# Even mixer of a two-block network: the gates' reciprocals in four pieces, the projection tiles in quarters over the recurrence's steps, and the logarithms of the attention's norm moved ahead

## The chip, the cores and the metric

The kernel runs on one core of a Trainium2 chip. The metric is the device time of one execution in microseconds (us), lower is better. TensorE (PE) has two levels of clock, 2.4 and 1.2 GHz; the profile gives the level granted in a stretch as a share, 1.00 or 0.50. DVE is VectorE, ACT is ScalarE, POOL is GpSimd.

## The reference, cut to what matters

The whole network is two blocks; the change lies in the even mixer of the second (512 tokens, width 1024, everything float32). Cut to what matters here:

```
def even_mixer(x, w_in, w_out, ...):
    h = x @ w_in
    qa, ka, va, hq, hf, hi, hg = jnp.split(h, cuts, axis=-1)
    o_a = diff_attention(qa, ka, va, ...)      # ends in an rms_norm * (1 - 0.2)
    o_b = hgrn2(hq, hf, hi, hg, lb, hg_g)
    return jnp.concatenate([o_a, o_b], axis=-1) @ w_out

def hgrn2(hq, hf, hi, hg, lb, out_g):          # 4 heads, chunks of 64 tokens
    ...
    a = einsum('nbhtk,nbhsk->nbhts', qc * exp(b - b_mid), kc * exp(b_mid - b))
    a = where(tril, a, 0)
    o_intra = einsum('nbhts,nbhsv->nbhtv', a, vc)
    def step(state, xs):                       # 8 chunks, one after the other
        o_inter = einsum('bhtk,bhkv->bhtv', qo, state)
        state = dc[..., None] * state + einsum('bhsk,bhsv->bhkv', ks, vv)
    ...
    o = rms_norm(o, out_g) * silu(hg)
```

`silu(hg)` is hg / (1 + exp(-hg)); this is "the gate" below.

## The kernel before

Each engine has a program of its own (`even_pe`, `even_act`, `even_dve`, `even_pool`), written out by hand; an engine works strictly in the order of its program, and semaphores (`wait_ge`, `then_inc`) join them. No scheduler moves anything.

**Projection.** `x @ w_in` is done in 28 tiles t = 0 to 27 (128 output columns x 512 tokens), each of 24 matmuls: 8 parts k of the inner dimension times three products (high and low halves of weights and input). Before a tile's matmuls ACT makes the high half of its weights (`act_hi`, L242) and DVE the low half (`dve_lo`, L249). `ev_tile` does a tile in one go, `ev_half(t, h)` does one half of it (12 matmuls, L3214 to L3216). Tiles 20, 21, 24, 25 are the values `hi` of heads 0 to 3, tiles 22, 23, 26, 27 the gates `hg`. A tile lands in a PSUM bank (`ev_bank`: B[6], or B[7]), and the next tile of that bank waits until it has been read. Values go to SBUF by ACT (`values`), are turned by PE (`ev_vtr`) and copied by DVE (`turn`).

**Gates.** `gates(t)`: ACT computes exp(-g) from PSUM into the buffer `vt` (L3499). DVE adds one (L3691), takes the reciprocal of the whole 128x512 tile (L3693) and multiplies by the tile in PSUM into `hg` (L3695), which frees the bank.

**The attention's norm.** PE has summed the squares of the four attention heads into banks B[0] to B[3]. ACT takes the logarithm (L3533) and then exp(-0.5 ...) (L3538); DVE scales the heads with it (L3765, L3768). The banks B[0] to B[5] are also those of the recurrence, so PE waits for the fourth logarithm (`da_ac.at("ln", 3)`) before the recurrence.

**Recurrence.** `hgrn` runs two heads side by side, first heads 0 and 1 (steps s = 1 to 9), then heads 2 and 3 (s = 1 to 11; steps 10 and 11 of heads 0 and 1, their norms, come right behind step 1 of the second pair). `head(h, 0)` prepares a head: two subtractions on DVE (L3718, L3720), five exponentials on ACT, four products on DVE (L3723 to L3727), three memsets. Step 1: PE turns the keys (L3379), ACT copies them (`kst`, L3470), PE forms the first two score blocks (L3366, L3367), DVE copies their lower triangles (`intra`, L3711, L3713). Step s = 2 to 9 is chunk c = s - 2: PE multiplies keys and values (L3390), score block and values (L3395) and the state and queries (L3397); DVE updates the state `sh` (L3743); ACT copies the output (L3475). At s = 3, 5 and 7 (odd steps below) PE also forms the next two score blocks, and DVE copies their triangles (four copies a head); the second of these blocks waits for the bank which the state update of the same step frees:

```
            elif 2 <= s < 10:
                ...
                if c % 2 and c < 7:
                    intra(c + 1)
                    intra(c + 2)
```

After the heads' parts of each step every engine calls its `between(s)` (first pair) or the second function (second pair), where other work is put. Before the change PE does half a tile at each of s = 2 to 9, tiles 24 to 27. ACT and DVE prepare heads 2 and 3 at s = 3 and s = 5. The gates 26 and 27 are whole on DVE at s = 8 and 9. The second pair has nothing beside it on PE and DVE; ACT copies parts of the result into `xh` (L3562), and POOL makes `xl` of six of them (L3792). Then come norms (L3408), the last products (L3750, L3753), and the output projection `pj_evo` (L257 to L259).

## Time and profile before

| what | value |
|---|---|
| median of 3 runs | 3791.18 us (3788.5 to 3801.71) |
| the profiled execution's own time | 3791.59 us |
| its span | 3789.8 us |
| granted TensorE clock, mean over the span | 0.952 |
| PE busy / weight loads busy | 3436.3 us (91%) / 2733.8 us (72%) |
| DVE / ACT / POOL busy | 2059.0 (54%) / 1491.5 (39%) / 224.9 us (6%) |

The stretch that the change touches is about 119 us long: it runs from the end of tile 23 at 2408.2 us to the first matmul of the output projection at 2526.97 us. The rows further down are read like this: a row of a timeline gives start, duration, engine, line, operation, output <- inputs, and in brackets how long the engine stood idle before it and whose end it waited for.

### The profile page before, as it was taken

Reading aid. Unit: us, or ns where it says so; the run is one execution under the profiler, and the core shown is the slowest. Engines: PE = TensorE matmul, PEld = TensorE weight load, DVE = VectorE, ACT = ScalarE, POOL = GpSimd, SP = SyncE. Lnnn points to the kernel's source line nnn. Section 1 sums busy time; section 2 is a strip of 40 time slices with the busy share of each in tenths; the row PEclk is TensorE's granted clock in tenths of the full one; section 3 lists DMA queues with packets and bytes.
Section 4 is the critical chain, followed back from the end, with each engine's and each line's share of the span. In section 5 each row is a group of like instructions: output and inputs, shape, how many; then the busy total and the mean of one; then the engine's idle time right before and its main releaser. Section 6 shows DMA issues by size and latency. Waiting matters only on the chain.

```text
span 3789.8 us, 59831 instructions
## 1 busy us (share of the span) xinstructions
PE 3436.3 (91%) x24660; PEld 2733.8 (72%) x24660; DVE 2059.0 (54%) x3388; ACT 1491.5 (39%) x2714; POOL 224.9 (6%) x455
## 2 busy tenths in 40 slices
PE   6888899999989958778899999789999989799999
PEld 4755788888866647676688887566888666568886
DVE  4377443334476747774544456655445655454446
ACT  5478342222246533334433334424333534343334
POOL 0011000000000014333100000000000000000000
PEclk8999999999999968999999999879999999899999
DMA  4122123321134677764222221111222211112221
GB/s 191 45 79 90 57 111 141 137 100 67 56 112 144 173 192 173 170 165 148 78 90 99 100 100 67 37 62 67 100 100 89 77 66 45 50 67 91 98 100 56
DMA packets 294414, 378.22 MB, mean 100 GB/s; under 512 B 240449, under 2 KB 243393, under 8 KB 259585
## 3 DMA queue, kind: packets, MB, share of 16 engines
q1 hardware_dynamic: 280912, 328.78, 27.0%
q10 hardware_dynamic: 13232, 45.61, 3.6%
q8 instruction: 198, 3.24, 0.4%
q14 instruction: 72, 0.58, 0.0%
HBM read 330.30 MB, written 44.06 MB: 99 GB/s over the span
## 4 chain that ended last, share of the span: by engine, by line
PE 79%; DVE 9%; ACT 6%; issue 3%; DMA 2%; POOL 0%; SPq 0%; ACTq 0%; DVEq 0%; POOLq 0%
PE ps L257 19%; PE ps L258 18%; PE ps L259 18%; PE ps L1368 1%; PE ps L1370 1%; PE ps L1369 1%; PE ps L339 1%; DVE wlo L249 1%; PE ps L803 1%; PE ps L789 1%; PE ps L2889 1%; PE ps L2213 1%; PE ps L2195 1%; PE ps L2223 1%; PE ps L3877 1%
## 5 line engine op out<-in xcount | busy, mean ns | idle before, releaser
L242 ACT ACTIVATE whi<-panel 128x512 fp32r<-128x512 f32 (+1 forms) x517 | 435.2, 842 | 585.7 <-PE ps L259 574.0
L249 DVE TENSOR_TENSOR wlo<-panel,whi 128x512 fp32r<-128x512 f32 (+1 forms) x517 | 495.8, 960 | 235.5 <-ACT whi L242 226.2
L257 PE MATMUL ps<-dh,whi 128*128 128x512 f32 (+1 forms) x1280 | 474.6, 371 | 0.0
L258 PE MATMUL ps<-dh,wlo 128*128 128x512 f32 (+1 forms) x1280 | 471.7, 369 | 0.0
L259 PE MATMUL ps<-dl,whi 128*128 128x512 f32 (+1 forms) x1280 | 471.4, 368 | 0.0
L257 PE MATMUL ps<-xh,whi 128*128 128x512 f32 x1088 | 443.2, 407 | 25.1 <-DVE xl L2930 19.2
L258 PE MATMUL ps<-xh,wlo 128*128 128x512 f32 x1088 | 429.2, 395 | 0.0
L259 PE MATMUL ps<-xl,whi 128*128 128x512 f32 x1088 | 428.8, 394 | 0.0
L257 PE MATMUL ps<-hh,whi 128*128 128x512 f32 (+1 forms) x960 | 352.8, 367 | 26.0 <-DVE hl L460 25.9
L258 PE MATMUL ps<-hh,wlo 128*128 128x512 f32 (+1 forms) x960 | 340.3, 354 | 0.0
L259 PE MATMUL ps<-hl,whi 128*128 128x512 f32 (+1 forms) x960 | 339.8, 354 | 0.0
L1161 DVE TENSOR_TENSOR relu<-relu 128x512 f32<-128x512 f32 (+1 forms) x160 | 102.2, 639 | 367.4 <-ACT relu L1136 367.4
L257 PEld LDWEIGHTS ps<-dh,whi 128*128 128x128 f32 x1280 | 241.4, 189 | 46.6 <-issue 3.3
L257 PEld LDWEIGHTS ps<-xh,whi 128*128 128x128 f32 x1088 | 207.6, 191 | 88.1 <-issue 23.0
L259 PEld LDWEIGHTS ps<-dl,whi 128*128 128x128 f32 x1280 | 241.3, 189 | 40.6
L258 PEld LDWEIGHTS ps<-dh,wlo 128*128 128x128 f32 x1280 | 241.5, 189 | 40.2
L1136 ACT ACTIVATE relu<-ps 128x512 f32<-128x512 f32 (+1 forms) x160 | 88.7, 554 | 427.6 <-PE ps L259 427.6
L258 PEld LDWEIGHTS ps<-xh,wlo 128*128 128x128 f32 x1088 | 208.3, 191 | 45.8 <-issue 5.1
L259 PEld LDWEIGHTS ps<-xl,whi 128*128 128x128 f32 x1088 | 207.6, 191 | 44.2
L257 PEld LDWEIGHTS ps<-hh,whi 128*128 128x128 f32 x960 | 183.4, 191 | 67.1 <-issue 27.7
L258 PEld LDWEIGHTS ps<-hh,wlo 128*128 128x128 f32 x960 | 184.3, 192 | 27.6 <-issue 4.6
L259 PEld LDWEIGHTS ps<-hl,whi 128*128 128x128 f32 x960 | 183.9, 192 | 25.1
(537 smaller groups left out, 5763.7 us busy)
## 6 DMA issues: line engine op xcount, KB each, us to landing
panel<-in_w SPq DMA_DIRECT2D x246, 1024.0 KB, 4.8
late<-s_fe ACTq DMA_DIRECT2D x16, 1024.0 KB, 5.7
late<-s_fe ACTq DMA_DIRECT2D x48, 256.0 KB, 3.9
s_fe<-x SPq DMA_DIRECT2D x24, 256.0 KB, 3.3
late<-s_fe ACTq DMA_DIRECT2D x8, 768.0 KB, 6.2
s_fe<-xx SPq DMA_DIRECT2D x16, 256.0 KB, 2.7
s_fe<-ctx SPq DMA_DIRECT2D x24, 128.0 KB, 2.9
s_ia<-panel SPq DMA_DIRECT2D x24, 128.0 KB, 4.0
```

The lines of the kernel that those rows point to most:

```text
L242: e.activation(unit(u)[0][:, 0:kc, :], w, ACT.Copy).then_inc(*w_hi.up(u))
L249: e.tensor_tensor(lo[:, 0:kc, :], w, hi[:, 0:kc, :].bitcast(F32), SUB).then_inc(*w_lo.up(u))
L257: e.matmul(out, hi[:, k, :], xh, start=k == 0, stop=False)
L258: e.matmul(out, lo[:, k, :], xh, start=False, stop=False)
L259: last = e.matmul(out, hi[:, k, :], xl, start=False, stop=k == kc - 1)
L339: i = e.matmul(ada_bank(n)[32 * j:32 * j + 32, 0:256], SCW[:, 2 * k:2 * k + 32], w[:, k * 256:k * 256 + 256], start=k < 4, stop=k > 3)
L789: x = e.transpose(B[4 + t % 2][:, i * P:i * P + P], S4[n % 3][:, i, j * P:j * P + P], ID)
L803: x = e.matmul(B[6][HALF[g % 2], :], VT[:, blocks[j], 64 * g:64 * g + 64], att_pt(n, j)[:, :], start=j == 0, stop=j == len(blocks) - 1)
L1136: e.activation(r, B[t % 6][:, 0:n], ACT.Relu).then_inc(*self.ac.up("relu", f))
L1161: e.tensor_tensor(r, r, r, MUL).then_inc(*self.dv.up("sq", f))
L1368: e.matmul(out, hi[:, k, :], xh, start=k == 0, stop=False)
L1369: e.matmul(out, lo[:, k, :], xh, start=False, stop=False)
```

## The change

1. **Gates.** ACT first copies the tile from PSUM to `hg` (`plain`, signal "raw"), which frees the bank; exp(-g) is then taken from `hg` into new buffers `ge`. DVE's `gates(t, *parts)` is cut up: "one", the reciprocals of four 128x128 pieces 0 to 3, and "mul", which now reads SBUF alone. The parts of gates 22 and 23 are spread over steps 2 to 9 of the first pair, those of 26 and 27 over steps 3 to 9 of the second.
2. **Projection tiles.** Half of tile 24 goes between step 1 of head 0 and step 1 of head 1, the other half behind step 1. Tiles 25 and 26 are done in quarters (6 matmuls) at s = 2 to 9, tile 27 in quarters at s = 2 to 5 of the second pair.
3. **Logarithms first.** ACT takes the four logarithms (L3533) before it prepares head 1.
4. **DVE's order.** The split of tile 25 and the scaling of the attention heads move behind step 1 and into steps 1 and 2. Head 2 is prepared at s = 3 and 4, head 3 at s = 6 and 7 (subtractions, then "s"). `act_hi`, `dve_lo`, `turn` move with their tiles.

The core of the diff:

```diff
@@ even_pe and its helpers @@
-    def ev_half(e, t, h):
+    def ev_half(e, t, h, n=4):
...
-        for k in range(4 * h, 4 * h + 4):
+        for k in range(n * h, n * h + n):
...
         def between(s):
-            if s in (5, 7):
-                ev_vtr(e, 22 + (s - 1) // 2)
-            if 2 <= s < 10:
-                ev_half(e, 24 + (s - 2) // 2, s % 2)
+            if s in (4, 7):
+                ev_vtr(e, 24 + s // 7)
+            if s == 1:
+                ev_half(e, 24, 1)
+            else:
+                ev_half(e, 25 + (s - 2) // 4, (s - 2) % 4, 2)
+
+        def second(s):
+            if 2 <= s < 6:
+                ev_half(e, 27, s - 2, 2)
...
             if s == 1:
+                if h == 1:
+                    ev_half(e, 24, 0)
...
@@ even_act @@
+        def plain(t):
+            e.wait_ge(*ev_mm.at("unit", EU + t))
+            e.activation(HG[:, ev_head(t), :], ev_bank(t)[:, :], ACT.Copy).then_inc(*ev_ac.up("raw", t))
+
         def gates(t):
-
-            e.wait_ge(*ev_mm.at("unit", EU + t))
-            e.wait_ge(*ev_mm.at("vtr", t - 2))
-            e.activation(VT2[t % 2][:, :], ev_bank(t)[:, :], ACT.Exp, scale=-1.0).then_inc(*ev_ac.up("sig", t))
+            if t > 23:
+                e.wait_ge(*ev_dv.at("tile", t - 4))
+            e.wait_ge(*ev_ac.at("raw", t))
+            e.activation(GE[t % 2][:, :], HG[:, ev_head(t), :], ACT.Exp, scale=-1.0).then_inc(*ev_ac.up("sig", t))
...
         act_hi(e, EU + 24)
-        gates(22)
-        head(1, 0)
         for h in range(4):
             e.wait_ge(*da_mm.at("sum", h))
             e.activation(RQ[h], B[h][:, :], ACT.Ln, scale=1.0 / 128, bias=vec("e5")).then_inc(*da_ac.up("ln", h))
+        plain(22)
+        head(1, 0)
         act_hi(e, EU + 25)
+        plain(23)
+        gates(22)
         gates(23)
...
@@ even_dve @@
-        def gates(t):
...
+        def gates(t, *parts):
+            g, d = GE[t % 2], HG[:, ev_head(t), :]
+            for part in parts:
+                if part == "one":
+                    e.wait_ge(*ev_ac.at("sig", t))
+                    e.tensor_scalar(g[:, :], g[:, :], 1.0, None, ADD).then_inc(*ev_dv.up("one", t))
+                elif part == "mul":
+                    e.wait_ge(*ev_dv.at("rec", t, 3))
+                    e.tensor_tensor(d, d, g[:, :], MUL).then_inc(*ev_dv.up("tile", t))
+                else:
+                    e.wait_ge(*ev_dv.at("one", t))
+                    e.reciprocal(g[:, part * P:part * P + P], g[:, part * P:part * P + P]).then_inc(*ev_dv.up("rec", t, part))
...
         def between(s):
-            if s in (5, 7):
-                dve_lo(e, EU + 24 + (s - 1) // 2)
-                turn(21 + (s + 1) // 2)
-            if s == 8:
...
+            if s == 1:
+                dve_lo(e, EU + 25)
+                scaled(0)
+                scaled(1)
+            elif s == 2:
+                scaled(2)
+                scaled(3)
+                gates(22, "one")
+            elif s == 3:
+                head(2, 0)
+                gates(22, 0)
+            elif s == 4:
+                head(2, "s")
+                gates(22, 1)
+            elif s == 5:
+                turn(24)
+                dve_lo(e, EU + 26)
+                gates(22, 2)
+            elif s == 6:
+                head(3, 0)
+                gates(22, 3, "mul")
+            elif s == 7:
+                head(3, "s")
+            elif s == 8:
+                turn(25)
+                dve_lo(e, EU + 27)
+                gates(23, "one", 0)
+            elif s == 9:
+                gates(23, 1, 2, 3, "mul")
+
+        def second(s):
+            if s == 2:
                 dve_lo(e, EU + 28)
-                gates(26)
-            if s == 9:
+            elif s == 3:
+                gates(26, "one", 0)
+            elif s == 4:
+                gates(26, 1, 2)
+            elif s == 5:
+                gates(26, 3, "mul")
+            elif s == 6:
                 dve_lo(e, EU + 29)
...
+            elif s > 6 and s < 10:
+                gates(27, *{7: ("one", 0), 8: (1, 2), 9: (3, "mul")}[s])
```

Three places of the order in which the engines work. First ACT, from the split of tile 24 on (L3462 to L3467 are the exponentials of head 1, `k` its buffer; `cs`, `mk`, `rt` hold the attention's norms), before:

```order
L242 ACTIVATE whi<-panel 128x1024
L3499 ACTIVATE vt<-ps 128x512
L3462 ACTIVATE k<-k 128x512
L3463 ACTIVATE k<-k 128x512
L3464 ACTIVATE k<-q 128x512
L3466 ACTIVATE k<-k 128x512
L3467 ACTIVATE dc<-q 128x8
L3533 ACTIVATE cs<-ps,vec 128x512 x2
L3533 ACTIVATE mk<-ps,vec 128x512
L3533 ACTIVATE rt<-ps,vec 128x512
L242 ACTIVATE whi<-panel 128x1024
```

and with the change:

```order
L242 ACTIVATE whi<-panel 128x1024
L3545 ACTIVATE cs<-ps,vec 128x512 x2
L3545 ACTIVATE mk<-ps,vec 128x512
L3545 ACTIVATE rt<-ps,vec 128x512
L3507 ACTIVATE hg<-ps 128x512
L3475 ACTIVATE k<-k 128x512
L3476 ACTIVATE k<-k 128x512
L3477 ACTIVATE k<-q 128x512
L3479 ACTIVATE k<-k 128x512
L3480 ACTIVATE dc<-q 128x8
L242 ACTIVATE whi<-panel 128x1024
L3507 ACTIVATE hg<-ps 128x512
```

The four logarithms (L3533, now L3545) stand ahead of head 1, and a plain copy of tile 22 (L3507) where the exponential of the gate stood.

Second DVE, from the last memset of head 1 on (L3765 and L3768 scale the attention's heads), before:

```order
L3686 MEMSET aa 128x64
L3691 TENSOR_SCALAR vt<-vt 128x512
L3693 RECIPROCAL vt<-vt 128x512
L3695 TENSOR_TENSOR hg<-ps,vt 128x512
L249 TENSOR_TENSOR wlo<-panel,whi 128x1024
L3691 TENSOR_SCALAR vt<-vt 128x512
L3693 RECIPROCAL vt<-vt 128x512
L3695 TENSOR_TENSOR hg<-ps,vt 128x512
L3765 SCALAR_TENSOR_TENSOR om<-om,vec,cs 128x512
L3768 TENSOR_SCALAR om<-om 128x512
```

and with the change, from the last of the eight triangle copies (L3737, L3739) on, which now follow the memset directly:

```order
L3737 COPY_PREDICATED aa<-mu,ps 32x64
L3739 COPY_PREDICATED aa<-mu,ps 32x32
L249 TENSOR_TENSOR wlo<-panel,whi 128x1024
L3792 SCALAR_TENSOR_TENSOR om<-om,vec,cs 128x512
L3795 TENSOR_SCALAR om<-om 128x512
L3792 SCALAR_TENSOR_TENSOR om<-om,vec,cs 128x512
L3795 TENSOR_SCALAR om<-om 128x512
L3770 SCALAR_TENSOR_TENSOR sh<-sh,dc,ps 128x128 x2
```

No reciprocal stands ahead of the first state updates (L3770) any more, and two of the four scalings are behind them.

Third DVE in the first pair, steps 5 and 6 (from the last triangle copy of step 5 on; `lf` is the buffer of head 3), before:

```order
L3713 COPY_PREDICATED aa<-mu,ps 32x32
L249 TENSOR_TENSOR wlo<-panel,whi 128x1024
L3587 COPY v<-ps 128x4x128
L3718 TENSOR_TENSOR lf<-q 128x512
L3720 TENSOR_TENSOR lf<-q 128x512
L3723 TENSOR_TENSOR lf<-lf,qh 128x512
L3724 TENSOR_TENSOR lf<-lf,kh 128x512
L3726 TENSOR_TENSOR lf<-lf,kh 128x512
L3727 TENSOR_TENSOR lf<-lf,qh 128x512
L3743 SCALAR_TENSOR_TENSOR sh<-sh,dc,ps 128x128 x3
```

and with the change:

```order
L3739 COPY_PREDICATED aa<-mu,ps 32x32
L3609 COPY v<-ps 128x4x128
L249 TENSOR_TENSOR wlo<-panel,whi 128x1024
L3721 RECIPROCAL ge<-ge 128x128
L3770 SCALAR_TENSOR_TENSOR sh<-sh,dc,ps 128x128 x2
L3744 TENSOR_TENSOR lf<-q 128x512
L3746 TENSOR_TENSOR lf<-q 128x512
L3721 RECIPROCAL ge<-ge 128x128
L3718 TENSOR_TENSOR hg<-hg,ge 128x512
L3770 SCALAR_TENSOR_TENSOR sh<-sh,dc,ps 128x128
```

Pieces of the reciprocal stand in both steps now, and head 3 is prepared over two steps instead of at once.

## Rows read from the trace of the kernel before

**Rows 1.** The page, chain that ended last, share of the span by engine.

```profile
PE 79%; DVE 9%; ACT 6%; issue 3%; DMA 2%; POOL 0%; SPq 0%; ACTq 0%; DVEq 0%; POOLq 0%
```

**Rows 2.** Stretches: us, PE, PEld, DVE, ACT, POOL busy (count), clock, DMA share, GB/s.

```profile
2408.20:2428.26 20.06, 3.74 (x27) 2.36 (x27) 19.11 (x28) 9.07 (x17) 0.00 (x0) 0.57 0.15 53
2428.26:2479.36 51.10, 47.76 (x242) 36.97 (x243) 27.08 (x65) 13.18 (x33) 0.00 (x0) 0.87 0.06 21
2479.36:2491.63 12.27, 6.30 (x43) 3.68 (x41) 11.59 (x23) 6.20 (x12) 1.35 (x1) 0.91 0.25 87
2491.63:2519.60 27.97, 26.69 (x126) 20.96 (x126) 9.54 (x38) 5.49 (x18) 6.33 (x5) 0.50 0.00 1
2519.60:2526.97 7.37, 3.47 (x5) 1.21 (x5) 2.94 (x5) 4.59 (x9) 0.00 (x0) 0.73 0.00 0
```

**Rows 3.** Timeline of DVE, from head 1's end to the first state update.

```profile
2413.23 0.37 DVE L3691 TENSOR_SCALAR vt<-vt 128x512 f32<-128x512 f32 x1
2413.63 3.35 DVE L3693 RECIPROCAL vt<-vt 128x512 f32<-128x512 f32 x1
...
2417.62 1.22 DVE L249 TENSOR_TENSOR wlo<-panel,whi 128x1024 fp32r<-128x1024 f32 x1
...
2423.20 0.74 DVE L3765 SCALAR_TENSOR_TENSOR om<-om,vec,cs 128x512 f32<-128x512 f32 x1
...
2429.63 0.35 DVE L3743 SCALAR_TENSOR_TENSOR sh<-sh,dc,ps 128x128 f32<-128x128 f32 x1
```

**Rows 4.** Timeline of PE, keys of head 0 turned, first product of step 2.

```profile
2413.99 1.11 PE L3379 MATMUL ps<-cst,tq 128*128 128x128 f32 x4 [5.70 <-ACT rt L3533]
...
2428.26 0.66 PE L3395 MATMUL ps<-aa,v 64*128 64x64 f32 x2 [9.42 <-DVE aa L3713]
```

**Rows 5.** Timeline of ACT, head 1's first exponential and the logarithms.

```profile
2409.34 0.63 ACT L3462 ACTIVATE k<-k 128x512 f32<-128x512 f32 x1 [2.55 <-DVE k L3718]
...
2411.55 1.24 ACT L3533 ACTIVATE cs<-ps,vec 128x512 f32<-128x512 f32 x2
```

**Rows 6.** Timeline of DVE, first pair, first updates of steps 3, 5, 7.

```profile
2436.77 0.35 DVE L3743 SCALAR_TENSOR_TENSOR sh<-sh,dc,ps 128x128 f32<-128x128 f32 x1 [5.13 <-PE ps L3397]
...
2439.76 0.69 DVE L3718 TENSOR_TENSOR cs<-q 128x512 f32<-128x512 f32 x1
...
2450.51 0.35 DVE L3743 SCALAR_TENSOR_TENSOR sh<-sh,dc,ps 128x128 f32<-128x128 f32 x1 [5.71 <-PE ps L3397]
...
2463.19 0.35 DVE L3743 SCALAR_TENSOR_TENSOR sh<-sh,dc,ps 128x128 f32<-128x128 f32 x1 [2.91 <-PE ps L3397]
```

**Rows 7.** Timeline of PE, head 1 in step 3, half tile, step 4.

```profile
2437.40 0.48 PE L3390 MATMUL ps<-v,kst 64*128 64x128 f32 x2
...
2439.14 0.50 PE L3214 MATMUL ps<-xh,whi 128*128 128x512 f32 x1
...
2442.09 0.49 PE L3390 MATMUL ps<-v,kst 64*128 64x128 f32 x2
...
2443.04 0.49 PE L3390 MATMUL ps<-v,kst 64*128 64x128 f32 x2
```

**Rows 8.** Groups by line and form of DVE: the smallest reciprocal.

```profile
L946 DVE RECIPROCAL nsm<-nsm 128x1 f32<-128x1 f32 x96 | 15.2, 158 | 11.6 <-ACT s L851 11.3
```

**Rows 9.** Timeline of DVE, second pair, first updates of steps 3 and 5.

```profile
2493.43 0.35 DVE L3743 SCALAR_TENSOR_TENSOR sh<-sh,dc,ps 128x128 f32<-128x128 f32 x1 [1.20 <-PE ps L3397]
...
2501.91 0.35 DVE L3743 SCALAR_TENSOR_TENSOR sh<-sh,dc,ps 128x128 f32<-128x128 f32 x1 [1.31 <-PE ps L3397]
```

**Rows 10.** Stretches of step 4 in the first pair, columns as rows 2.

```profile
2442.00:2445.00 3.00, 2.20 (x14) 1.78 (x14) 2.77 (x6) 1.91 (x7) 0.00 (x0) 1.00 0.00 0
2445.00:2448.00 3.00, 3.00 (x8) 2.33 (x9) 0.00 (x0) 0.75 (x1) 0.00 (x0) 0.51 0.00 0
```

**Rows 11.** Timeline, POOL and DVE at the second pair's start.

```profile
2488.98 1.35 POOL L3792 TENSOR_TENSOR xl<-om,xh 128x512 fp32r<-128x512 f32 x1 [668.65 <-ACT xh L3562]
2489.12 1.75 DVE L3750 SCALAR_TENSOR_TENSOR om<-om,vec,k 128x512 f32<-128x512 f32 x1
```

More of the change, by code:

```diff
@@ L3402, in head @@
             elif s == 11:
-                if h < 2:
-                    e.wait_ge(*ev_dv.at("tile", 26 + h))
+                if h == 0:
+                    e.wait_ge(*ev_ac.at("raw", 26))
+                elif h == 1:
+                    e.wait_ge(*ev_dv.at("v", 25))
+                elif h == 2:
+                    e.wait_ge(*hg_ac.at("norm", 0, 0))
                 else:
-                    e.wait_ge(*hg_ac.at("norm", h - 2, 0))
+                    e.wait_ge(*ev_ac.at("raw", 27))
                 e.wait_ge(*hg_ac.at("sq", h))
                 e.matmul(B[6 + x_][:, :], ONES, QP, start=True, stop=True).then_inc(*hg_mm.up("norm", h))
-        hgrn(head, between, nothing)
+        hgrn(head, between, second)
         after(e, hg_ac, hg_dv)
@@ L3562, in parts @@
                 e.activation(EXH[:, k, :], EOM[:, k, :], ACT.Copy).then_inc(*ev_ac.up("hi", k))
-        hgrn(head, between, parts)
+        hgrn(head, between, second)
         for k in range(6, 8):
@@ L3756, in even_dve @@
         head(0, 0)
+        head(0, "s")
         turn(21)
@@ L3759, in even_dve, with scaled @@
         head(1, 0)
-        gates(22)
-        dve_lo(e, EU + 25)
-        gates(23)
-        for h in range(4):
+        head(1, "s")
+        def scaled(h):
             e.wait_ge(*da_ac.at("r", h))
```

60 lines of the change are left out of this document (28 added, 32 removed).

## The prediction

> **What bounds the kernel now.** I read the page first: the chain that ended last is PE for 79% of the span and DVE for 9% [rows 1]. Over the whole kernel PE is the bound, but the change lies in 119 us in which it is not, so I then read the stretches of those 119 us [rows 2]. The reader should see four regimes. In the 20.06 us before the first pair of heads PE is busy for 3.74 us and DVE for 19.11: DVE is the bound. In the first pair (51.10 us) PE is busy for 47.76 and DVE for 27.08: PE is the bound and DVE has 24 us to spare. In the 12.27 us between the pairs DVE is the bound again (11.59). In the second pair (27.97 us) PE is busy for 26.69, but its clock is 0.50: it crawls through small matmuls at 1.2 GHz. The last 7.37 us are a chain through all engines.
>
> Next the timelines say what holds PE. It waits 5.70 us for the attention's last logarithm before it may turn head 0's keys, then 9.42 us for the triangle copies of DVE, which stand behind both gates and all scalings [rows 4]; a whole reciprocal takes 3.35 us [rows 3]. ACT sits idle for 2.55 us ahead of head 1's exponentials, with the logarithms queued behind them [rows 5].
>
> **The change part by part.** I follow marks, each the start of an instruction, before against after.
>
> *Up to the first pair.* The logarithms start in ACT's gap, at 2409.34 - 2.55 = 2406.8 less the 0.5 us of the old gate exponential: 2406.25. Four at 0.57 us (two take 1.24 [rows 5]) end at 2408.6, and the copy of tile 22 at 2409.1, before head 1's exponentials may start at 2409.34: they move nothing. PE's banks are free at 2408.6 instead of 2413.9. PE does head 0's step 1 (0.8 us at full clock), half of tile 24 (12 matmuls, 2.95 us by [rows 7], 2442.09 - 2439.14), then waits until head 1 is ready on DVE at 2413.23 [rows 3], does its step 1 and the other half of tile 24: 2416.9. Behind head 1, ACT has a split (0.95), a copy, two gate exponentials, four exponentials of the norm (0.52 each) and the key copy: head 0's keys are there at 2416.7. So PE starts step 2 at about 2416.9, its first mask product at 2417.2 instead of 2428.26 [rows 4]. DVE, from 2413.23 on: eight triangle copies 2.0, split of tile 25 1.13, two scalings 1.15 each (0.74 + 0.43, [rows 3]): its first state update comes at 2418.7 instead of 2429.63 [rows 3]. **11 us gained.** A whole tile of PE work has also moved out of the first pair.
>
> *First pair, DVE's side.* After it DVE has two scalings (2.3), one add (0.4) and two updates (0.6) before step 3: 2422.0 instead of 2436.77 [rows 6]. The price of a piece of a reciprocal is not in the trace; it is bounded from below by 3.35 / 4 = 0.84 [rows 3] and from above by that plus the whole 0.158 us of the smallest one [rows 8], 1.0. A line through 158 ns and 3352 ns gives 0.95 for 128 columns, and I take that; twelve more instructions then cost DVE 1.8 us in all. An odd step holds DVE and PE together for 3.0 us (2439.76 - 2436.77, [rows 6]), since PE's next score block waits for the update. An even step's two updates take 0.6. A 128x512 product starts 0.6 us after the one before it. So DVE needs
> - steps 3 and 4: 3.0 + (1.2 + 0.95) + 0.6 + (2.4 + 0.95) = 9.1
> - steps 5 and 6: 3.0 + (0.6 + 1.13 + 0.95) + 0.6 + (1.2 + 0.95 + 0.6) = 9.0
> - steps 7 and 8: 3.0 + 2.4 + 0.6 + (0.6 + 1.13 + 0.35 + 0.95) = 9.0
>
> *First pair, PE's side.* At full clock a head costs 1.74 us in an odd step (2439.14 - 2437.40) and 0.95 in an even one (2443.04 - 2442.09), and a quarter tile half of 2.95 [rows 7]: 2 x 1.74 + 2 x 0.95 + 2 x 1.45 = 8.3 for two steps. So **DVE becomes the bound**, at 9.0 us for two steps; before, they took 13.74 and 12.68 [rows 6]. Step 3 at 2422.0, step 5 at 2431.1, step 7 at 2440.1, DVE done with step 8 at 2449.1. PE does step 9 and the last quarter of tile 26 meanwhile, ready at 2449.8; before, tile 27 ended at 2479.36 [rows 2]. Now **29.6 us gained**.
>
> *Between the pairs.* DVE has the rest of gate 23 (3 x 0.95 + 0.6 = 3.5) until 2452.6, two resets with triangle copies (2.8), the last products of heads 0 and 1 (2.8): the second pair's first update at 2458.2 instead of 2491.63 [rows 2]. PE's key turns and norms and ACT's squares, logarithms and exponentials end by 2455.8 and hide behind it. **33.4 us gained**, the largest sum on the way.
>
> *Second pair.* New here are four quarters of tile 27 on PE and two splits and two gates on DVE. DVE needs 6.2 to 6.7 us for two steps. PE, at 1.2 GHz, took 8.48 (2501.91 - 2493.43, [rows 9]); the two quarters add 2.9 at full clock or 5.9 at half. At full clock steps 3 and 4 are 8.3 us, at half clock 14.4. I take full clock while the quarters run (steps 2 to 5) and half after: 8.3 + (3.5 + 1.5 + 3.3) + 8.5 for steps 3 to 8, plus 1.8 for the split of tile 28 ahead of step 3, is 26.9 from the first update, and 0.8 for step 9: 27.7, against 27.97 before [rows 2]. The quarters cost nothing then, because they carry the clock.
>
> *The end* stays as it was (7.37 us); ACT's sixth part of `xh` moves to step 10 but hides behind PE's norm. The panels of weights are asked for by the splits, which all come earlier in absolute time and stand well ahead of their tiles: no cost, no gain.
>
> **The sum** is 33.4 + 0.3 = 34 us if the clock stays up. It will not all the way. The rows show that it falls inside the first pair too: after a stretch with little beside recurrence matmuls and a short wait (2.20 of 3.00 us busy) it is 0.51 [rows 10], and the pair's mean is 0.87 [rows 2]. With quarters in place of halves and DVE as the bound, recurrence-only stretches come at every step. I allow 2 us there, 2 in the second pair and 1 for POOL (below): 29 us. The profiled execution took 3791.6 us, 0.4 above the median of the runs, so **3762 us** is forecast for either.
>
> A rule of the Trainium skill speaks against the change: "TensorE: Matmul & The Clock Gate", section on the second failure mode, says that a PE that idles briefly but often between groups of matmuls makes its clock go up and down, and loses throughput that way. By it the first rival would be the case.
>
> **Rivals.**
>
> *1. The clock goes up and down in the first pair.* For: [rows 10]; the second pair at 0.50 throughout [rows 2] shows that recurrence matmuls alone do not lift it. Against: quarters are more evenly spread than halves, and 0.87 was held before with PE busy for no larger a share. At half clock PE needs 2 x 8.3 less the waits in it, about 14.4 us for two steps, against DVE's 9.0. If half of the stretches are at half clock, two steps take some 11.5: 3 x 2.5 = 7.5 us lost, and 6 in the second pair, where steps 3 and 4 take 14.4. The gain is 34 - 13.5 = 20 us or less: 3771 to 3780.
>
> *2. The clock falls before step 2 and does not come back until the output projection* (the side of slower). Its place is the wait before head 1's step 1. Each half of tile 24 then takes 5.9 us (+6), steps 2 to 9 take 3 x 14.4 + 10 instead of about 33 (+20), key turns, norms and step 2 between the pairs +4, steps 3 to 8 of the second pair 14.4 + 11.4 + 8.5 instead of 25.1 (+9). With step 1's own +1 that is 40 us lost of 34 gained: 6 us slower, 3798. It decides once more than about seven eighths of the stretch is at 1.2 GHz. Against: 12 full-width matmuls in a row stand there twice, and with such halves the first pair reached a mean of 0.87 from a start at half clock [rows 2].
>
> *3. DVE's pieces cost more than I take*, or POOL holds it up. One DVE product took 1.75 us instead of 0.75 beside a POOL subtraction [rows 11]; six of these now run at steps 5 to 10 beside pieces and products: at most 6 us, most of it in PE's shadow. With 1.0 a piece and waits of 0.2 at each step, 5 us more. Gain 23 to 25 us: 3767.
>
> *4. The gain does not show,* because PE is the bound before and after and only waits move. Against: PE's busy time in the stretch falls only by what runs faster, but the idle time in [rows 4] (15.1 us) is on the chain and does go. 3786 or more would be this.
>
> **How the numbers follow.** What a measurement of this kernel can tell from no change is 0.5%, 19 us. Forecast (clock mostly high, 24 to 38 us gained): 0.58. Rival 3: 0.14, still over 19 us faster. Rival 1: 0.19, of which a quarter is just beyond 19 us. Rival 2: 0.04, and rival 4: 0.05. Faster by over 0.5%: 0.58 + 0.14 + a little of rival 1 = 0.75; within 0.5%: 0.21; slower: 0.04, for a rival 2 with more behind it than I see. The range: below, the second pair wholly at full clock (8.3 + 6.9 + 6.7, 4 us less) gives 34 + 4 = 38 us, 3753; above, rival 1 at its worst with DVE's pieces at their upper bound, about 10 us gained, 3782.
>
> **What would show it right or wrong.** PE should turn head 0's keys at about 2408.7 us and start the first mask product near 2417; DVE's first updates of steps 3, 5 and 7 should lie 9 us apart, with idle times on PE that end with DVE's update; the pieces should take about 0.95 us each. The second pair's first update should come near 2458, the output projection's first matmul near 2498 (2493 without the allowances). The forecast is wrong if steps 3 to 8 of the first pair take 35 us or more at a clock near 0.6, if the pieces take over 1.1 us, or if the second pair takes over 34 us.

## The result, and the profile after

The changed kernel takes **3770.59 us** (median of 4 runs, 3767.46 to 3772.44); the kernel before, run beside it, 3792.36 (4 runs, 3788.5 to 3801.71). The ratio is 0.9938, with a 95% interval of 0.9919 to 0.9958: 21.8 us or 0.6% faster, where 29 us and 3762 were forecast. In a second comparison the same kernel took 3767.94 against 3790.93 (0.9946, 0.9929 to 0.9964).

The profiled execution took 3772.44 us, with a span of 3770.3. I count from the start of the last matmul of tile 23 (2407.90 before, 2405.53 after), since what stands ahead of it is the same program in both, and call "the stretch" what lies between it and the output projection's first matmul. It took 119.1 us before and takes 101.9 now: 17.1 us less. The other 2.4 us of the 19.5 by which the spans differ lie ahead of the change. Times of the marks from that zero, with the forecast's marks put on the same zero:

| start of | before | forecast | after |
|---|---|---|---|
| head 0's keys turned (PE) | 6.1 | 0.8 | 0.8 |
| first state update (DVE) | 21.7 | 10.8 | 10.7 |
| first update of step 3 | 28.9 | 14.1 | 14.5 |
| of step 5 | 42.6 | 23.2 | 25.5 |
| of step 7 | 55.3 | 32.2 | 39.8 |
| second pair, first update | 83.7 | 50.3 | 61.7 |
| output projection (PE) | 119.1 | 85.1, or 90.1 with the allowances | 101.9 |

The forecast holds up to step 3 and falls behind at each mark after it. The stretches between the marks of the changed kernel (the columns of [rows 2]) show with what:

```profile
2406.29:2416.22 9.93, 9.27 (x59) 6.95 (x60) 8.96 (x24) 8.46 (x17) 0.00 (x0) 1.00 0.11 29
2420.04:2431.03 10.99, 9.84 (x60) 7.09 (x56) 8.21 (x21) 4.30 (x11) 0.00 (x0) 0.84 0.00 0
2431.03:2445.28 14.25, 13.01 (x52) 9.50 (x52) 8.36 (x21) 3.51 (x10) 0.00 (x0) 0.55 0.00 1
2445.28:2467.19 21.91, 20.14 (x111) 14.31 (x110) 16.78 (x42) 9.15 (x20) 0.00 (x0) 0.83 0.14 50
2468.85:2481.50 12.65, 12.11 (x52) 9.00 (x52) 5.97 (x18) 0.73 (x4) 0.00 (x0) 0.60 0.00 0
2481.50:2490.41 8.91, 8.06 (x50) 5.72 (x46) 5.63 (x16) 3.74 (x10) 0.58 (x1) 0.80 0.00 0
2490.41:2507.46 17.05, 12.07 (x42) 8.04 (x43) 10.87 (x24) 7.74 (x19) 7.67 (x6) 0.60 0.18 62
```

The first row is the front, and there PE and DVE are now both at work, where before PE had 3.74 us of work in 20.06 [rows 2]. Rows 2 and 3 are steps 3 and 4, and 5 and 6, of the first pair: PE is busy for 90% of them and DVE for 75% and 59%, so PE is still the bound over most of both, and not DVE. Row 3 says why: the granted clock is 0.55. In narrower stretches of the same pair:

```profile
2424.00:2427.00 3.00, 3.00 (x15) 2.05 (x13) 1.66 (x3) 2.39 (x6) 0.00 (x0) 0.75 0.00 0
2427.00:2430.00 3.00, 3.00 (x19) 2.39 (x18) 2.51 (x5) 1.18 (x2) 0.00 (x0) 1.00 0.00 0
2430.00:2433.00 3.00, 2.08 (x20) 1.41 (x19) 2.22 (x8) 0.45 (x2) 0.00 (x0) 0.89 0.00 0
2433.00:2436.00 3.00, 2.86 (x11) 2.01 (x10) 2.75 (x7) 0.00 (x0) 0.00 (x0) 0.50 0.00 0
2436.00:2439.00 3.00, 3.00 (x12) 2.35 (x10) 1.31 (x3) 0.22 (x1) 0.00 (x0) 0.50 0.00 0
```

The clock goes up, holds for a while and falls again after a stretch in which PE had idled for 0.92 us (busy 2.08 of 3.00). It is the picture of [rows 10], now once more in the first pair and again in the second. PE's timeline says whose end it had waited for, the state update of step 5 on DVE:

```profile
2431.33 0.24 PE L3373 MATMUL ps<-tq 128*32 128x64 f32 x1 [0.92 <-DVE sh L3770]
```

That update (2431.03, below) started without a wait of its own, right behind four products and a piece of a reciprocal. So at this one place of the first pair DVE did hold PE up, and the clock fell about 1 us after that wait (0.89 is the mean over 2430 to 2433). The second execution of the changed kernel (`e_again`, below) has no such wait there, and its clock was low already (0.60 in steps 3 and 4): the wait is not the only thing ahead of which the clock falls.

"TensorE: Matmul & The Clock Gate" of the Trainium skill, in its section on the second failure mode, has this up and down of a PE that idles briefly between groups of matmuls. The trace agrees: 0.84, 0.55 and 0.83 in the three stretches from step 3 to the second pair. That the change of PSUM banks is what makes the short waits, as the page has it, no run here shows; the wait above ended with DVE's update.

At the front, the waits of [rows 3, 4] are gone. PE's timeline, key turns of head 0 and first mask product of step 2 (last brackets: the idle time ahead and its releaser):

```profile
2406.29 0.65 PE L3388 MATMUL ps<-cst,tq 128*128 128x128 f32 x4 [0.37 <-ACT rt L3545]
...
2414.89 0.33 PE L3404 MATMUL ps<-aa,v 64*128 64x64 f32 x2
```

DVE's timeline, first update, a piece of a reciprocal, the first updates of steps 3, 5, 7 and 8, the last four pieces of gate 23 and the second pair's first update:

```profile
2416.22 0.76 DVE L3770 SCALAR_TENSOR_TENSOR sh<-sh,dc,ps 128x128 f32<-128x128 f32 x2
...
2420.04 0.35 DVE L3770 SCALAR_TENSOR_TENSOR sh<-sh,dc,ps 128x128 f32<-128x128 f32 x1 [0.49 <-PE ps L3406]
...
2424.36 0.94 DVE L3721 RECIPROCAL ge<-ge 128x128 f32<-128x128 f32 x1
...
2431.03 0.25 DVE L3770 SCALAR_TENSOR_TENSOR sh<-sh,dc,ps 128x128 f32<-128x128 f32 x1
...
2445.28 0.35 DVE L3770 SCALAR_TENSOR_TENSOR sh<-sh,dc,ps 128x128 f32<-128x128 f32 x1 [2.25 <-PE ps L3406]
...
2453.60 0.35 DVE L3770 SCALAR_TENSOR_TENSOR sh<-sh,dc,ps 128x128 f32<-128x128 f32 x1 [1.88 <-PE ps L3406]
...
2457.29 3.39 DVE L3721 RECIPROCAL ge<-ge 128x128 f32<-128x128 f32 x4
...
2467.19 0.61 DVE L3770 SCALAR_TENSOR_TENSOR sh<-sh,dc,ps 128x128 f32<-128x128 f32 x2
```

The reader is to see the brackets: ahead of the first updates of steps 7 and 8 DVE waits 2 us for PE's products, with gates and splits already behind it. Only the update of step 5 has no bracket. But for that one place DVE does not hold the pair up.

### The profile page after: what moved, and what is told of

Read it like the earlier page. It is cut to its first block, busy times and chain, and to the rows that moved or that the text cites. A ratio compares the mean times of both kernels' runs of the same rounds, so it can differ in the third digit from the quotient of the medians.

```text
span 3770.3 us, 59844 instructions
## 1 busy us (share of the span) xinstructions
PE 3441.4 (91%) x24660; PEld 2731.6 (72%) x24660; DVE 2057.3 (55%) x3400; ACT 1493.5 (40%) x2718; POOL 224.2 (6%) x455
## 4 chain that ended last, share of the span: by engine, by line
PE 80%; DVE 8%; ACT 6%; issue 3%; DMA 2%; POOL 0%; SPq 0%; ACTq 0%; DVEq 0%; POOLq 0%
PE ps L257 19%; PE ps L259 19%; PE ps L258 19%; PE ps L1368 1%; PE ps L1370 1%; PE ps L1369 1%; PE ps L339 1%; PE ps L803 1%; DVE wlo L249 1%; PE ps L789 1%; PE ps L2889 1%; PE ps L2195 1%; ACT s L851 1%; PE ps L2223 1%; PE ps L3215 1%
## 5 line engine op out<-in xcount | busy, mean ns | idle before, releaser
L259 PEld LDWEIGHTS ps<-dl,whi 128*128 128x128 f32 x1280 | 241.1, 188 | 40.8
L259 PEld LDWEIGHTS ps<-xl,whi 128*128 128x128 f32 x1088 | 207.5, 191 | 44.4
L259 PEld LDWEIGHTS ps<-hl,whi 128*128 128x128 f32 x960 | 183.9, 192 | 25.5
```

The source lines that it names most:

```text
L259: last = e.matmul(out, hi[:, k, :], xl, start=False, stop=k == kc - 1)
```

## The experiments

Three theories stood: **the clock** (A: PE at 1.2 GHz takes back what the front gave), **DVE** (B: pieces and gates spread over the steps are what costs), and **the front alone** (C: which of the three edits made the gain). Twelve kernels ran in three series, each on one chip with runs of the kernel before beside it. One profiled execution shows where the time of one run goes; the medians say what an edit is worth. The two don't always say the same here, and I keep them apart.

### Which edit made the gain

**Logarithms first, and nothing else** (`e_ln`, from the kernel before):

```diff
         act_hi(e, EU + 24)
-        gates(22)
-        head(1, 0)
         for h in range(4):
...
+        gates(22)
+        head(1, 0)
         act_hi(e, EU + 25)
```

> The kernel before, with one part of the change: the four logarithms of the attention's norm taken ahead of the gate 22 and head 1 on ACT. 'The stretch' is from the start of tile 23's last matmul to the output projection's first: 119.1 us before, 101.9 with the whole change. If the triangle copies of DVE end the wait (my reading), PE turns head 0's keys 5 us earlier and then waits as much longer: stretch 118 to 120, time within 2 us of before. If the wait of 5.7 us was on the chain by itself, the stretch is 113 to 115.

Measured: 3789.86 us against 3791.12, ratio 0.9998 (0.9988 to 1.0007). PE turned its keys at 0.8 us instead of 6.1, and the first update stayed where it was, at 21.7: PE no longer had the 5.70 us wait of [rows 4] and waited that much longer for DVE instead: 3.60 us for head 1's preparation, and 11.73 instead of 9.42 us for the triangle copies. The stretch was 118.4 us, as expected. This part of the change alone is worth nothing.

**Everything but the gates' move** (`e_gates_back`, from the changed kernel): both gates whole on DVE behind head 1's score scalings, as before the change.

```diff
+                elif part == "whole":
+                    e.wait_ge(*ev_dv.at("one", t))
+                    e.reciprocal(g[:, :], g[:, :]).then_inc(*ev_dv.up("rec", t, 3))
...
         head(1, "s")
+        gates(22, "one", "whole", "mul")
+        gates(23, "one", "whole", "mul")
...
-                gates(22, "one")
```

(and so for every other call of `gates(22, ...)` and `gates(23, ...)` in the steps.)

> The changed kernel with the gates 22 and 23 whole again on DVE ahead of the recurrence (2 x 4.46 = 8.9 us), all else as changed. Clock theory (in steps 5 to 9 PE at 1.2 GHz is the bound, DVE has slack): the first pair gets little shorter from the work taken off DVE, stretch 107 to 111. DVE theory (DVE's gate pieces set the steps): what is added ahead comes off the steps again, stretch 101 to 104. Besides, the late start lets the clock fall before step 2, which would add up to 3 us to either.

Measured: 3785.06 us against 3791.12, ratio 0.9986 (0.9976 to 0.9996). The first update came at 20.0 us instead of 10.7. So some 13 to 17 us of the gain hang on the gates' being away from the front: 16 to 17 by the changed kernel's two gains of 21.8 and 23.0 us, 13 by `e_whole`, which ran in the same series. All the rest of the change together brings about 6.

The stretch does not show this: it was 103.5 us, only 1.6 more than in the changed kernel's profile, and in the range that the expectation gave to DVE. Its steps 3 and 4 say that DVE was not the reason: without any piece they took 13.54 us at 0.57, with them 13.45 at 0.60 in `e_again`. The shorter steps came at full clock, 5 and 6 of the first pair and 3 and 4 of the second:

```profile
2446.45:2455.89 9.44, 8.10 (x56) 5.93 (x52) 5.99 (x17) 3.68 (x11) 0.00 (x0) 1.00 0.00 1
2478.21:2486.62 8.41, 7.75 (x52) 5.86 (x52) 5.92 (x17) 0.73 (x4) 0.00 (x0) 1.00 0.00 0
```

The profiled execution (3777.61 us) was also the second fastest of the ten. The verdict rests on the median.

**The reciprocals whole, at the same steps** (`e_whole`): tile 22's at step 6, tile 23's at step 9, tile 26's and 27's at steps 4 and 8 of the second pair.

```diff
             elif s == 6:
                 head(3, 0)
-                gates(22, 3, "mul")
+                gates(22, "whole", "mul")
...
             elif s == 9:
-                gates(23, 1, 2, 3, "mul")
+                gates(23, "whole", "mul")
```

> The changed kernel with each gate's four pieces in one reciprocal again (22 at step 6, 23 at 9, 26 at 4, 27 at 8), in the same stages. If cutting up is what lets them hide, PE waits some 2.5 us at step 6 and the triangle or state work behind it, and the clock falls for it: stretch 104 to 108. If DVE has slack at 1.2 GHz anyway, stretch 100.5 to 103, and DVE is 1.8 us less busy.

Measured: 3771.96 us against 3791.12, ratio 0.9948 (0.9933 to 0.9963). That is the changed kernel's time. What matters is that the reciprocals were moved; that they were cut into pieces brings nothing that can be measured. The stretch was 98.3 us, shorter than either expectation. PE did wait 2.58 us for the update behind tile 26's whole reciprocal in the second pair, and 0.75 us at step 7 of the first.

### Is DVE the bound?

**No reciprocals** (`e_norec`): the gates are multiplied by 1 + exp(-g) instead of its reciprocal, which leaves the sixteen pieces out of the computation. Their row among the changed kernel's groups by line (busy us, mean ns of one, idle time ahead):

```profile
L3721 DVE RECIPROCAL ge<-ge 128x128 f32<-128x128 f32 x16 | 14.3, 928 | 0.1
```

```diff
                 elif part == "mul":
-                    e.wait_ge(*ev_dv.at("rec", t, 3))
+                    e.wait_ge(*ev_dv.at("one", t))
                     e.tensor_tensor(d, d, g[:, :], MUL).then_inc(*ev_dv.up("tile", t))
-                else:
-                    e.wait_ge(*ev_dv.at("one", t))
-                    e.reciprocal(g[:, part * P:part * P + P], g[:, part * P:part * P + P]).then_inc(*ev_dv.up("rec", t, part))
```

> The changed kernel without the 16 pieces of reciprocals (the gates are multiplied by 1 + exp(-g), so their values are others; everything else runs). DVE theory: 15 us of DVE work gone, the first pair's steps 3 to 9 shorter by 0.9 each, the part between the pairs by 2.8: stretch 90 to 94. Clock theory: DVE waits longer for PE, only step 9 and the part between the pairs get shorter: stretch 96 to 100.

Measured: 3770.57 us against 3791.12, ratio 0.9949 (0.9934 to 0.9963). Run again beside the changed kernel itself (`e_norec_again`, the same text; `e_again` is the changed kernel without an edit):

> The kernel without reciprocals once more, now timed on the same chip as the changed one. If DVE set the steps, it is 8 to 12 us faster than the changed kernel in the same rounds. If it is PE and its clock, 0 to 5 us, the 2.5 to 3 us between the pairs being all that is sure.

> The changed kernel once more, as the reference of this call and as a second sample of where its clock falls. Clock theory: the stretch from tile 23's end to the output projection is 98 to 106 us and what differs from the first profile (101.9) lies in spans whose granted clock differs; spans at 1.00 repeat within 0.3 us. Time 20 to 24 us under before.

Measured: 3767.95 (0.9953, 0.9936 to 0.9971) and 3767.94 us (0.9946, 0.9929 to 0.9964), against 3790.93. **Taking 14.3 us of work from DVE does not change the medians.** The 8 to 12 us that the expectation asked of theory B are not there; a gain of some 5 us would not show in these few runs. So B falls as the main cause, by the medians. The profiles alone would have said otherwise: the stretches were 92.3 and 94.9 us without reciprocals (90 to 94 were expected for B) and 101.9 and 107.0 with them. But DVE was busy for only 75% of steps 3 and 4 of the changed kernel and 59% of steps 5 and 6, and those four executions had their clock in different places: 0.84 and 0.72 in steps 5 and 6 without reciprocals, 0.55 and 0.63 with them, 1.00 against 0.60 and 0.53 in steps 3 and 4 of the second pair. A middle way is open: without the piece ahead of step 5's update PE's wait of 0.92 us is gone too, and it may be by such waits that DVE's work moves the clock. No run here separates the two.

The changed kernel's second stretch, 107.0 us, lies 1 us beyond what was expected of it. The part between the pairs, at 1.00, repeats within 0.01 us (12.64 and 12.65).

The trace without reciprocals also tells which chain runs beside DVE's work between the pairs. DVE's timeline, and under it PE's:

```profile
2457.69 0.35 DVE L3767 SCALAR_TENSOR_TENSOR sh<-sh,dc,ps 128x128 f32<-128x128 f32 x1 [0.60 <-PE ps L3406]
...
2467.44 0.75 DVE L3774 SCALAR_TENSOR_TENSOR om<-om,vec,tq 128x512 f32<-128x512 f32 x1 [2.44 <-ACT tq L3498]
...
2470.34 0.61 DVE L3767 SCALAR_TENSOR_TENSOR sh<-sh,dc,ps 128x128 f32<-128x128 f32 x2
```

```profile
2464.93 1.10 PE L3421 MATMUL ps<-tq,cst 128*128 128x512 f32 x2 [1.48 <-ACT tq L3492]
```

From step 8's last update to the second pair's first it takes 12.65 us with DVE waiting 2.44 for ACT, against 12.64 (2454.55 to 2467.19) in the changed kernel, where DVE has no wait but 3.39 us of pieces there. Two chains end together: DVE's own work, and the outputs' norm through ACT's squares, PE's sums, ACT's logarithm and exponential. Shortening DVE's alone gave nothing here. For the other no run was made; in the changed kernel's trace DVE is free 0.1 us before ACT's last exponential ends, so little would come of it.

### Is it the clock?

**Idle matmuls in the first pair** (`e_fill1`): three more 512-column matmuls ahead of the quarter in six of the eight steps, into a bank that nobody reads then.

```diff
+        if more:
+            if t == 25 and h < 2:
+                e.wait_ge(*ev_ac.at("raw", 23))
+            for _ in range(more):
+                e.matmul(B[7][:, :], hi[:, 0, :], hi[:, 0:4, :].rearrange("p a b -> p (a b)"), start=True, stop=True)
...
+                ev_half(e, t, h, 2, 0 if s in (5, 8) else 3)
```

(and the tiles' turns behind the quarter, with waits that keep the bank apart.)

> The changed kernel with three idle matmuls of 512 columns (0.23 us each at 2.4 GHz, into a bank nobody reads) ahead of the quarter tile at steps 2, 3, 4, 6, 7 and 9 of the first pair: 18 matmuls, 4.1 us at full clock, 7.7 at half. Clock theory: they keep the clock at 2.4 GHz in the first pair, and it gets shorter although PE has more to do: from the first update of step 3 to the second pair's first update 39 to 43 us, 47.2 in the changed kernel's profile. If the clock is a consequence and not the cause, they add 4 to 8 us.

Measured: 3771.83 us against 3793.98, ratio 0.9933 (0.9916 to 0.9950). The first pair, steps 3 and 4, then 5 and 6, then step 7 to the second pair, and the second pair's steps 3 and 4, in its profiled execution:

```profile
2430.32:2440.55 10.23, 9.70 (x66) 7.48 (x62) 8.20 (x20) 4.03 (x11) 0.00 (x0) 1.00 0.00 0
2440.55:2450.67 10.12, 8.74 (x59) 6.50 (x55) 8.21 (x21) 3.67 (x11) 0.00 (x0) 1.00 0.01 2
2450.67:2471.16 20.49, 18.48 (x117) 13.38 (x114) 16.66 (x42) 9.15 (x20) 0.00 (x0) 1.00 0.14 52
2472.82:2485.25 12.43, 11.76 (x52) 8.77 (x52) 5.92 (x18) 0.73 (x4) 0.00 (x0) 0.63 0.00 0
```

Work that computes nothing, 18 matmuls of it, makes the first pair shorter: 40.8 us from step 3 to the second pair against 47.2. So theory A holds for where the time goes in this pair, in this one execution. Without reciprocals the same stretch took 41.8 and 44.2 us, and 44.4 in `e_whole`, all without a fill: part of the 6 us may be where the clock fell and not the fill. And the whole kernel gains nothing that can be told (22.2 us under before, against 21.8 and 23.0 without the fill). The second pair, at 0.63 and then 0.50, took 42.9 us from its first update instead of 40.3.

**Idle matmuls in the second pair** (`e_fill2`): four behind each of steps 3 to 9.

```diff
+            if 3 <= s < 10:
+                if s == 3:
+                    e.wait_ge(*w_lo.at(EU + 28))
+                idle(28, B[6], 4)
```

> The changed kernel with four such idle matmuls behind each of steps 3 to 9 of the second pair (28, 6.4 us at full clock, 12 at half). From the second pair's first update to the output projection the changed kernel takes 40.3 us. Clock theory: 35 to 38, at a clock near 1.00, steps 5 and 6 no more than 9 us. Otherwise 44 to 50.

Measured: 3778.81 us against 3793.98, ratio 0.9962 (0.9948 to 0.9976): some 7 us slower than the changed kernel by their gains over before. The stretch was 103.9 us in its profiled execution, and the second pair took 43.7 us to the projection, where 35 to 38 were expected. A miss as a whole, but not in every part: with the tile's quarters the fill makes ten wide matmuls in each of steps 3 to 5, and there the clock did come up. From the second pair's first update to the end of step 4, and from there to the end of step 6:

```profile
2469.35:2480.43 11.08, 10.21 (x50) 7.53 (x50) 5.34 (x17) 0.73 (x4) 0.00 (x0) 0.69 0.00 0
2480.43:2490.67 10.24, 9.71 (x61) 7.37 (x60) 6.17 (x16) 3.38 (x9) 0.00 (x0) 1.00 0.01 2
```

Steps 5 and 6 took 9.23 us, where no more than 9 were expected. The clock was lower again behind them (0.69 to the projection), with the four alone. What the fill costs is more than what it lifts.

**Nine matmuls per step, nothing beside the second pair** (`e_nine`): tiles 25 to 27 go through the eight steps of the first pair three k-blocks at a time, in two banks by turns, and the DVE and ACT parts move with them.

```diff
+    def ev_part(e, i):
+        t, k = 25 + i // 8, i % 8
...
             else:
-                ev_half(e, 25 + (s - 2) // 4, (s - 2) % 4, 2)
+                for i in range(3):
+                    ev_part(e, 3 * (s - 2) + i)
...
         def second(s):
-            if 2 <= s < 6:
-                ev_half(e, 27, s - 2, 2)
+            pass
```

> The changed kernel with tile 27 also in the first pair: tiles 25 to 27 as nine matmuls at each of steps 2 to 9, nothing on PE beside the second pair; DVE's splits, turns and gate pieces moved to suit. Real work in the filler's place. Clock theory: the first pair stays at 0.95 and more and becomes PE-bound near 9.9 us for two steps, so from step 3's first update to the second pair's first 44 to 48 us with a whole tile more in it; second pair as before the change, 8.5 us for two steps, 35.3 to the projection. Stretch 95 to 100. If the extra tile simply costs what it takes at the present mean clock, stretch 102 to 106.

> The kernel with nine matmuls of tiles 25 to 27 at each step of the first pair, against the changed one in the same rounds: 4 to 9 us faster than it, stretch 91 to 96, granted clock 0.95 or more from step 3 of the first pair to the second pair's first update, and 0.50 in the second pair.

Measured: 3765.13 us against 3793.98, ratio 0.9926 (0.9910 to 0.9942), and again 3766.27 against 3790.93, 0.9934 (0.9922 to 0.9945). Steps 3 and 4, 5 and 6, step 7 to the second pair, and the second pair's steps 3 and 4, in the first profiled execution:

```profile
2420.69:2432.44 11.75, 11.22 (x66) 8.64 (x62) 7.62 (x18) 3.78 (x11) 0.00 (x0) 0.85 0.00 0
2432.44:2442.73 10.29, 9.76 (x66) 7.37 (x62) 9.40 (x22) 1.95 (x6) 0.00 (x0) 1.00 0.01 2
2442.73:2463.05 20.32, 17.48 (x108) 12.59 (x107) 15.95 (x44) 11.40 (x26) 0.00 (x0) 1.00 0.14 53
2464.70:2473.45 8.75, 8.19 (x41) 6.46 (x40) 5.89 (x17) 0.89 (x4) 0.00 (x0) 0.50 0.00 0
```

With half as much useful work again in each step, the first pair holds its clock better and is shorter than with quarters: 42.4 and 42.3 us from step 3 to the second pair, against 47.2 and 48.2. It fell for a short while once in either execution (0.85 is the mean of steps 3 and 4 here, 0.79 that of steps 7 and 8 in the other). The second pair, at half clock and with nothing beside it, takes 8.75 us for two steps instead of 12.65. The stretch is 92.7 and 92.4 us, 9 to 15 us shorter than the changed kernel's two, and shorter than the 95 to 100 expected at first. The medians lie 28.9 and 24.7 us under before, where the changed kernel's lie 21.8 and 23.0. It is the fastest version of the study by its medians and beats the kernel before in both of its series; from the changed kernel the intervals do not separate it. Beside it, in one series, it was 1.7 us faster, where 4 to 9 were expected: a miss.

**The same, with four idle matmuls in each step of the second pair** (`e_nine_fill`; DVE's split of tile 28 comes a step earlier as well):

```diff
         def second(s):
-            pass
+            if 2 <= s < 10:
...
+                idle(28, B[6], 4)
```

> The former with four idle matmuls behind each of steps 2 to 9 of the second pair. Clock theory: second pair at full clock, 7.2 us for two steps instead of 8.5, 31 to 33 us from its first update to the projection; stretch 92 to 96, the shortest of all. Otherwise 8 x 1.7 us longer than the former: 108 or more.

Measured: 3780.37 us against 3793.98, ratio 0.9962 (0.9949 to 0.9975), some 15 us slower than without the fill, and 49.0 us from the second pair's first update to the projection, where 31 to 33 were expected. The two stretches of the second pair, steps 3 and 4 and steps 5 and 6:

```profile
2470.90:2483.19 12.29, 12.01 (x52) 8.70 (x50) 6.03 (x16) 0.89 (x5) 0.00 (x0) 0.50 0.00 0
2483.19:2495.48 12.29, 12.00 (x52) 8.70 (x50) 6.24 (x16) 2.88 (x8) 3.11 (x2) 0.50 0.07 15
```

PE is busy for 98% of the time here, at a clock of 0.50 throughout. Four matmuls of 512 columns in each step did not lift the clock in 24.6 us, where the ten per step of `e_fill2` were followed by 1.00. Each two steps grew by 3.5 us for eight of them. The nine of the first pair held a clock that was already up, which is another thing.

**Halves instead of quarters** (`e_halves`): tiles 25 and 26 in halves at steps 3, 5, 7 and 9, tile 27 at steps 3 and 5 of the second pair, the rest as in the changed kernel.

```diff
-            else:
-                ev_half(e, 25 + (s - 2) // 4, (s - 2) % 4, 2)
+            elif s % 2:
+                ev_half(e, 25 + (s - 3) // 4, (s - 3) // 2 % 2)
```

> The changed kernel with the tiles 25 and 26 in halves at steps 3, 5, 7 and 9 and tile 27 in halves at steps 3 and 5 of the second pair, nothing at even steps: the same work in bigger lumps. If an even spread is what holds the clock, it falls more often: first pair 3 to 6 us longer than in the changed kernel, time 3 to 8 us longer. If only the amount counts, the same within 2 us.

Measured: 3776.74 us against 3790.93, ratio 0.9966 (0.9953 to 0.9979), 8.8 us over the changed kernel in the same series; the two intervals overlap. Steps 3 and 4, and 5 and 6:

```profile
2417.30:2430.61 13.31, 10.77 (x56) 8.16 (x56) 8.26 (x21) 4.14 (x10) 0.00 (x0) 0.76 0.00 0
2430.61:2443.56 12.95, 10.53 (x52) 7.95 (x52) 8.28 (x20) 3.23 (x8) 0.00 (x0) 0.74 0.01 2
```

The same matmuls in bigger lumps leave PE busy for 81% in place of about 90%, at a mean clock of 0.75. PE waits 2.15, 2.31 and 2.37 us for DVE's update at steps 3, 5 and 7, with no half in the even step before to cover the wait. The clock is not lower than in the changed kernel's two executions (0.84 and 0.55, 0.60 and 0.63), so it is not what the spread wins. From step 3 to the second pair it took 49.4 us (47.2 and 48.2 in the changed kernel), a smaller difference than the 3 to 6 us expected. That even spreading is worth some 9 us is likely by the medians and not shown.

## Why the prediction was right, and where it was off

**Right: the front.** 11 us were forecast up to the first update and 11.0 came (21.7 to 10.7). The logarithms cost ACT's other work nothing, PE's keys were turned at the forecast 0.8 us, and the gates' reciprocals had stood on the path: giving them their place back takes some 13 to 17 us of the gain. At step 3 the gain was 14.4 of the forecast 14.8.

**Luck: that the time lies in the range.** The gain of 21.8 us is outside the 24 to 38 of the forecast proper; the range holds it because its upper end was set by rival 1 at its worst. The sum itself, 34 us less 5, rests on a first pair that DVE bounds and on a second pair at full clock while the quarters run, and neither came.

**Right: the prices.** A piece of a reciprocal took 0.94 to 0.95 us by its row, and 3.39 for four in a row; 0.95 was forecast. The full-clock and half-clock prices of two steps with their quarters held as well. For 8.3 us there were 8.41 (`e_norec`, second pair, clock 1.00). For 14.4 there were 14.25 at 0.55, and 13.83 at 0.53 in the second pair of `e_again`. What failed was which of them applies.

**Wrong: "DVE becomes the bound, at 9.0 us for two steps".** At full clock two steps of the first pair took 10.2 and 10.1 with idle matmuls beside them and 9.44 in `e_gates_back`, without pieces. The first pair of `e_fill2` is the changed kernel's own; there steps 3 and 4 ran at 1.00 and took 9.57 us, with PE waiting 0.92 us for DVE's update: near the 9.1 forecast. In the changed kernel's profile they took 11.0 and 14.25, with PE busy for 90% of them. The step from "PE needs 8.3 at full clock" to "so DVE bounds it" took for granted a clock that the changed kernel does not hold. The test of it is the runs without reciprocals: no change in the medians. The cost was 7.1 us between the marks of steps 3 and 7, of which up to 2.3 are not the clock's (20.35 us at 1.00 in `e_fill1`, against 18.1).

**Wrong: between the pairs.** From step 7's update to the second pair 18.1 us were forecast and 21.9 came; at a clock of 1.00, `e_fill1` and `e_nine`, which have more matmuls in them, still took 20.5 and 20.3. Of the 3.8 us missing up to 2 are thus not the clock but the term's size: to step 8's last update it took 7.15 us at full clock (`e_fill1`, with its fill) where 6.0 was in the sum, and the norm's chain, which I had "hide behind" DVE, ends about when DVE's does. The rest is the clock.

**Only sometimes right: the quarters "cost nothing then, because they carry the clock".** The second pair took 40.3 us from its first update to the projection, and 44.3 in the other execution of the changed kernel, instead of the forecast 34.8; before, without any quarter, it took 35.3. Its steps 3 and 4 ran at 0.60 and 0.53. In `e_gates_back`, whose second pair is the same program, and in both runs of `e_norec` they ran at 1.00 and took 8.41 us, and the pair 36.1 to 36.3 us. So the quarters can run at full clock and then cost about 1 us; nothing in them makes sure of it. At 0.60 two of them cost 4.2 us (12.65 less the 8.48 of [rows 9]). `e_nine` has no quarter there and took 36.2 us at half clock: as good as the best case, without the risk. In `e_nine_fill` four wide matmuls per step did not fetch the clock back; in `e_fill2` ten did, at a price that was higher than what came of it.

**The sum.** It was 34 us without allowances; off it come 7.1, 3.8 and 5.5 us for the three terms and 0.4 up to step 3, which leaves the 17 us by which the profiled stretch is shorter. I had allowed 5. Of the 17 lost, up to 2.3, 2.4 and 1.3 us and the 0.4 are terms sized too small even at full clock; the rest, 10.5 us and more, is put down to the clock. The two profiled executions differ by 19.2 us and the medians by 21.8. **Rival 1 is what happened**, priced at two steps of 11.5 us (12.6 measured, the mean of 11.0 and 14.25) and at a gain of 20 us or less; the median lies 0.4 us outside its 3771 to 3780, between it and the forecast's 24 to 38. It deserved more than 0.19, since both pieces of evidence for it, [rows 10] and the 0.50 in [rows 2], were in the trace. Rival 2 (the clock low all along) did not come: from the keys to the first update it was 1.00. Rival 3's waits for POOL are small: the second pair's first subtraction on POOL took 1.79 us instead of 1.26 and the split on DVE beside it its usual 1.23; further on DVE's addition of one for gate 27 took 0.94 us beside a subtraction, where gate 26's took 0.43. Rival 4 falls with the time itself. (In the range's lower end, 8.3 + 6.9 + 6.7 is 3.2 us less than 25.1, not 4; it moves that end by less than 1 us.)

**The signs.** The pieces' price and the marks up to step 3 came as said. The updates of steps 3, 5 and 7 did not lie 9 us apart (11.0 and 14.25), and an idle time of PE of over 0.3 us that ends with DVE's update came once in those steps and not at each. Steps 3 to 8 of the first pair, up to their last update, took 34.5 us at a mean clock near 0.65, and 35.6 near 0.6 in `e_again`: by the forecast's own sign (35 us or more near 0.6) its account of the pair fails in one execution and all but fails in the other.

Still open is why the medians of `e_norec`, `e_fill1` and the changed kernel agree while their profiled stretches differ by 3 to 15 us. The profiles say where such a difference can hide. What lies behind the stretch took 1262.8 to 1265.1 us in all fourteen, but what lies ahead of it, the same program each time, 2403.4 to 2415.1. In the profile of `e_norec` tile 23 ended 8.5 us later than in the changed kernel's, and that took back most of a stretch 9.6 us shorter: the two spans differ by 1.0 us. A median of four to six runs carries this spread too. That the stretch is shorter in `e_nine` is seen twice; that its time is, is likely and not shown.

## What to carry to other kernels

When work is moved so that an engine gets it earlier, price what stands behind the first mark at both levels of PE's clock, with rows of the same kind of work at either level, and not by the mean of a stretch that is to be rebuilt. Of two places for the same wide matmuls, try first the one in which the clock is already up: in `e_nine` it mostly stayed up with them, while beside matmuls at half clock each cost 0.44 us (3.5 for eight) instead of 0.23. And leave a suspect's work out before a schedule is built around it: two sets of runs showed that the reciprocals, once away from the front, no longer mattered for the median time.

## What was not expected of the hardware

**One program, several timetables.** The changed kernel's six runs in one series went from 3762.11 to 3785.21 us, and its two profiled executions had stretches of 101.9 and 107.0 us. Steps 3 and 4 of the first pair in the second of them, beside 10.99 us at 0.84 in the first:

```profile
2426.02:2439.47 13.45, 12.92 (x60) 9.71 (x56) 8.30 (x21) 4.14 (x11) 0.00 (x0) 0.60 0.00 0
```

The instructions and their order are the same; the clock fell at another place. Also the point at which tile 23 ends, with the same matmuls ahead of it, lay between 2403.4 and 2415.1 us in the fourteen profiles. A gain of 5 us in one profiled stretch of this kernel, or of 10 in one profiled time, is thus within what the same program does by itself, and only the medians of several runs carry a verdict.

**PE can be busy throughout and stay at half clock.** In `e_nine_fill` it was 98% busy for 24.6 us, with 16 matmuls of 512 columns and the recurrence's small ones, and the clock stayed at 0.50.
